# One recurrence, four engines: who takes the raw scores out of PSUM in the chunked RWKV-7 time mix

## What is computed

```python
def rwkv7_step(state, inp):
    r, w, k, v, a, bb = inp
    sa = jnp.einsum('bhij,bhj->bhi', state, a)
    state = (state * w[:, :, None, :] + sa[..., None] * bb[:, :, None, :]
             + v[..., None] * k[:, :, None, :])
    y = jnp.einsum('bhij,bhj->bhi', state, r)
    return state, y
```

## Time and profile before

| quantity | value |
| --- | --- |
| median of 3 runs | 3548.25 us |
| the profiled execution, its own time | 3558.19 us |
| its span in the profile | 3556.3 us |
| busy share of the span: TensorE, VectorE, ScalarE, GpSimd | 94%, 44%, 42%, 66% |
| mean granted clock of TensorE | 0.965 |
| recurrence (four chunks) | about 426 to 585 us |
| TensorE busy in one chunk of 38.8 us (third) | 29.7 us |
| GpSimd busy in the recurrence | 0 us |

### The profile page before, as it was taken

The page is one execution under the profiler, slowest core; times in us unless marked ns, Lnnn a source line. Parts: engine busy times, 40 slices in busy tenths (PEclk is TensorE's granted clock), DMA queues, the critical chain, the costliest instruction groups (busy, mean ns, idle before and its releaser), DMA issues.

```text
span 3556.3 us, 64623 instructions
## 1 busy us (share of the span) xinstructions
PE 3326.2 (94%) x23774; PEld 2994.4 (84%) x23774; DVE 1568.0 (44%) x2801; ACT 1476.6 (42%) x1933; POOL 2362.5 (66%) x1013
## 2 busy tenths in 40 slices
PE   7899878899999999888688999999999999999999
PEld 6798777888888888787677999998888888888899
DVE  2057755312221100369922495667741575137600
ACT  3255433444444333444344454343344334433433
POOL 5620101688888788553366787777788778877787
PEclk9999889999999999898899999999999999999999
DMA  5843301556555555443244555555555555655555
GB/s 179 194 151 129 109 3 61 155 173 187 184 187 184 174 186 184 132 130 95 71 136 144 164 183 166 170 171 154 176 171 186 172 173 161 194 177 172 159 183 165
DMA packets 158083, 555.26 MB, mean 156 GB/s; under 512 B 17248, under 2 KB 23584, under 8 KB 157840
## 3 DMA queue, kind: packets, MB, share of 16 engines
q1 hardware_dynamic: 151008, 540.08, 48.3%
q0 software_dynamic: 2192, 8.20, 1.3%
q10 hardware_dynamic: 4768, 5.36, 0.5%
HBM read 548.33 MB, written 5.24 MB: 156 GB/s over the span
## 4 chain that ended last, share of the span: by engine, by line
PE 74%; DVE 10%; POOL 8%; issue 7%; ACT 1%; POOLq 0%; DVEq 0%; ACTq 0%
PE ps L543 27%; PE ps L534 24%; PE ps L545 14%; POOL wl L482 8%; DVE ps L1704 2%; PE ps L743 2%; PE ps L612 1%; PE ps L936 1%; PE ps L570 1%; DVE arena L1673 1%; DVE misc L1671 0%; DVE under_u L1342 0%; DVE ehl L1841 0%; PE ps L621 0%; DVE arena L1495 0%
## 5 line engine op out<-in xcount | busy, mean ns | idle before, releaser
L482 POOL TENSOR_TENSOR wl<-raw,wh 128x1024 fp32r<-128x1024 f32 x984 | 2348.2, 2391 | 1059.7 <-ACT wh L1020 1059.6
L1020 ACT ACTIVATE wh<-raw 128x1024 fp32r<-128x1024 f32 (+1 forms) x1034 | 1087.1, 1053 | 1687.3 <-PE ps L545 1152.3
L543 PE MATMUL ps<-uhl,wh 128*128 128x512 f32 x3200 | 1140.9, 401 | 63.6 <-DVE uhl L1358 34.0
L534 PE MATMUL ps<-uhl,wh 128*128 128x256 f32 x4768 | 945.6, 289 | 19.4 <-DVE uhl L1358 9.9
L545 PE MATMUL ps<-uhl,wl 128*128 128x256 f32 x3200 | 903.6, 282 | 0.0
L534 PEld LDWEIGHTS ps<-uhl,wh 128*128 128x128 f32 x4768 | 777.0, 196 | 30.8 <-issue 12.4
L543 PEld LDWEIGHTS ps<-uhl,wh 128*128 128x128 f32 x3200 | 606.9, 190 | 215.7 <-DVE uhl L1358 35.2
L534 PE MATMUL ps<-uhl,wl 128*128 128x256 f32 x2640 | 754.6, 286 | 0.0
L545 PEld LDWEIGHTS ps<-uhl,wl 128*128 128x128 f32 x3200 | 610.7, 191 | 0.0
L543 PE MATMUL ps<-ehl,wh 128*128 128x512 f32 x1536 | 556.1, 402 | 9.2 <-DVE ehl L1841 5.6
L534 PEld LDWEIGHTS ps<-uhl,wl 128*128 128x128 f32 x2640 | 515.2, 195 | 0.0
(11 more groups left out here) (310 smaller groups left out, 2689.0 us busy)
## 6 DMA issues: line engine op xcount, KB each, us to landing
raw<-w_u SPq DMA_DIRECT2D x256, 512.0 KB, 3.5
raw<-w_v SPq DMA_DIRECT2D x256, 512.0 KB, 3.5
raw<-w_gu SPq DMA_DIRECT2D x176, 512.0 KB, 3.5
raw<-w_down SPq DMA_DIRECT2D x80, 512.0 KB, 3.6
raw<-w_out SPq DMA_DIRECT2D x64, 512.0 KB, 3.5
raw<-w_z SPq DMA_DIRECT2D x54, 512.0 KB, 3.7
raw<-w_in SPq DMA_DIRECT2D x52, 512.0 KB, 3.5
raw<-w_qkv SPq DMA_DIRECT2D x48, 512.0 KB, 3.6
```

Source lines behind the costliest of these rows:

```text
L482: pool.tensor_tensor(wl[:, slot, 0:width], raw[:, slot, 0:width], wh[:, slot, 0:width].bitcast(F32), ALU.subtract).then_inc(lo_ready, 1)
L534: ins = pe.matmul(out, w[:, slot, at], x(c), start=first and c == n == 0, stop=last and c == kt - 1 and n == 2)
L543: pe.matmul(bank(b).rearrange("p (n t) -> p n t", n=2), wh[:, slot, at], pair[:, :, k0 + c, :], start=first and c == 0, stop=False, skip_g ...
L1020: act.activation(wh[:, slot, 0:width], raw[:, slot, 0:width], ACT.Copy).then_inc(hi_ready, 1)
```

## The change

VectorE no longer masks the whole scores. It multiplies the near blocks straight from PSUM into `Bf[0]`, one instruction for each e over two banks, and then L727's product into `Bf[1]`. ScalarE waits for each of these near blocks and then copies the raw scores of that e, 128 x 1024, from PSUM to a new SBUF buffer `RAW`. It no longer makes the copy of v. GpSimd, between the fourth and the fifth split of `out`, runs a loop over the chunks: the identity added to the near blocks (`Bf[3]`), the far blocks (`Bf[2]`) from `RAW` in two instructions, the upper half of `QS` in two, the copy of v (not in the last chunk), and `MB` in two. TensorE gets waits at the places where each is first read, and `dve+` now takes its operand from the PSUM bank. `RAW` takes 2048 columns behind `MB`.

```diff
@@ -174,6 +174,7 @@
 ]
 PLUS_ID = {(2, 4), (6, 5)}
 NSTEP = len(INVERSE)
+FAR_STEP = min(n for n, step in enumerate(INVERSE) if any(2 in (a, b) for a, b, _, _ in step))
 
 
 MEAN_AT = (0, 2, 3, 5, 6, 8, 10, 11)
@@ -301,6 +302,7 @@
         o = temps
         QS = view(arena, o, NH, P); o += NH * P
         MB = view(arena, o, NH, P); o += NH * P
+        RAW = view(arena, o, 2, 8, P); o += 16 * P
         assert o <= temps_end, (o, temps_end)
         SV = view(xT_, 0, NH, CH)
         UV = view(xT_, 1024, NH, CH)
@@ -395,6 +397,9 @@
         p_ready, uh_ready = sem("p_ready"), sem("uh_ready")
         gp_ready, gh_ready = sem("gp_ready"), sem("gh_ready")
         gate_sum, up_sum, res_low, exp_sum = sem("gate_sum"), sem("up_sum"), sem("res_low"), sem("experts_sum")
+        scores_kept, near_in, near_id, far_in, qs_masked, v_low, mb_masked = (sem(n) for n in (
+            "scores_kept", "near_blocks", "near_plus_identity", "far_blocks", "reads_masked", "values_copied",
+            "keys_masked"))
         bk_tr, st_read, res_attn = sem("keys_turned"), sem("state_read"), sem("attention_added")
         mh_ready, ml_ready = sem("mixed_hi"), sem("mixed_lo")
         s_x = [sem(f"x_in{k}") for k in range(4)]
@@ -512,7 +517,31 @@
             for h in range(NH):
                 bias(h)
             pool.wait_ge(lo_ready, BASE["out"])
-            splits(BASE["out"], 32 + 176)
+            splits(BASE["out"], RING)
+            MB4, QS4 = (m.rearrange("p (k e) n -> p e k n", e=2) for m in (MB, QS))
+            wide = lambda m, n: m.unsqueeze(1).to_broadcast([CH, 8, n])
+            for c in range(NC_):
+                pool.wait_ge(near_in, 2 * c + 2)
+                pool.tensor_tensor(Bf[3], Bf[0], cst("i64").unsqueeze(1).to_broadcast([P, 8, CH]), ALU.add)\
+                    .then_inc(near_id, 1)
+                pool.wait_ge(near_id, c + 1)
+                for e in range(2):
+                    pool.wait_ge(scores_kept, 2 * c + e + 1)
+                    if e:
+                        pool.wait_ge(far_in, 2 * c + 1)
+                    pool.tensor_tensor(Bf[2][HD * e:HD * e + HD], RAW[0:CH, e, :, 0:CH], wide(cst("omask")[0:CH], CH),
+                                       ALU.mult).then_inc(far_in, 1)
+                pool.wait_ge(far_in, 2 * c + 2)
+                for e in range(2):
+                    pool.tensor_tensor(QS4[CH:P, e], RAW[CH:P, e], wide(cst("cmask")[CH:P], P), ALU.mult)\
+                        .then_inc(qs_masked, 1)
+                if c < NC_ - 1:
+                    pool.wait_ge(v_copied, c + 1)
+                    pool.tensor_copy(UV[CH:P, :, :], SV[CH:P, :, :]).then_inc(v_low, 1)
+                for e in range(2):
+                    pool.tensor_tensor(MB4[0:CH, e], RAW[0:CH, e], wide(cst("cmask")[0:CH], P), ALU.mult)\
+                        .then_inc(mb_masked, 1)
+            splits(BASE["out"] + RING, 32 - RING + 176)
             splits(BASE["down"], 96, 2 * DOWN_U, (DOWN_U - 1, 2 * DOWN_U - 1))
             splits(BASE["in2"], 4)
             pool.wait_ge(u_ready, 3 * DT)
@@ -720,7 +749,7 @@
                                         BK[hp:hp + HD, k, c, :], AR[hp:hp + HD, k, c, :], start=True, stop=True)
                     ins.then_inc(c_ps, 1)
 
-                pe.wait_ge(c_act, 5 * c + 2)
+                pe.wait_ge(c_act, 4 * c + 2)
                 for h in range(NH):
                     hp = HD * (h % 2)
                     k = h // 2
@@ -730,8 +759,13 @@
                 for n, step in enumerate(INVERSE):
                     if n == 0:
                         pe.wait_ge(c_dve, c + 1)
-                        pe.wait_ge(c_act, 5 * c + 5)
+                    if n == 1:
+                        pe.wait_ge(near_id, c + 1)
+                    if n == FAR_STEP:
+                        pe.wait_ge(far_in, 2 * c + 2)
                     for g in range(GROUPS):
+                        if n == 0 and g:
+                            pe.wait_ge(scores_kept, 2 * c + 2)
                         if evacuated(EVA, c, n, g):
                             pe.wait_ge(i_act, evacuated(EVA, c, n, g))
                         if evacuated(EVD, c, n, g):
@@ -748,6 +782,8 @@
 
                 if c:
                     pe.wait_ge(st_ev, c)
+                pe.wait_ge(c_act, 4 * c + 4)
+                pe.wait_ge(qs_masked, 2 * c + 2)
                 for g in range(GROUPS):
                     for h in range(8 * g, 8 * g + 8):
                         hp, k = HD * (h % 2), h // 2
@@ -766,11 +802,14 @@
                                         Bf[3][hp:hp + HD, k, :], start=True, stop=True)
                     ins.then_inc(v_ps, 1)
                 pe.wait_ge(uv_ev, GROUPS * (c + 1))
+                if c < NC_ - 1:
+                    pe.wait_ge(v_low, c + 1)
                 for h in range(NH) if c < NC_ - 1 else ():
                     ins = pe.matmul(bank(2 + h // 8)[0:CH, (h % 8) * CH:(h % 8 + 1) * CH], BKn[:, h, :],
                                     UV[:, h, :], start=True, stop=True)
                 if c < NC_ - 1:
                     ins.then_inc(n_ps, 1)
+                pe.wait_ge(mb_masked, 2 * c + 2)
                 for h in range(NH):
                     ins = pe.matmul(y_out(h), UV[0:CH, h, :], MB[0:CH, h, CH:P], start=False, stop=h >= NH - 2,
                                     skip_group_check=True)
@@ -1126,8 +1165,10 @@
                 for e in range(2):
                     act.activation(QS4[0:CH, e, :, :], AR4[HD * e:HD * e + HD, :, c, :], ACT.Copy)\
                         .then_inc(c_act, 1)
-                act.wait_ge(v_copied, c + 1)
-                act.activation(UV[CH:P, :, :], SV[CH:P, :, :], ACT.Copy).then_inc(c_act, 1)
+                for e in range(2):
+                    act.wait_ge(near_in, 2 * c + e + 1)
+                    act.activation(RAW[:, e], ps[:, 4 + 2 * e:6 + 2 * e, :].rearrange("p b (k n) -> p (b k) n", k=4),
+                                   ACT.Copy).then_inc(scores_kept, 1)
                 for n, step in enumerate(INVERSE):
                     for g in range(GROUPS):
                         half = slice(4 * g, 4 * g + 4)
@@ -1476,10 +1517,8 @@
             wend2 = wendh.rearrange("p (k e) n -> p e k n", e=2)
             dve.tensor_copy(wend2[0:HD, 0, :, :], wend[0:HD, :, :])
             link(dve.tensor_copy(wend2[0:HD, 1, :, :], wend[HD:P, :, :]))
-            MB4 = MB.rearrange("p (k e) n -> p e k n", e=2)
-            QS4 = QS.rearrange("p (k e) n -> p e k n", e=2)
             UV4 = UV.rearrange("p (k e) n -> p e k n", e=2)
-            cm, i64 = cst("cmask"), cst("i64")
+            i64 = cst("i64")
             for c in range(NC_):
                 dve.wait_ge(c_tr, c + 1)
                 if c == 0:
@@ -1490,23 +1529,12 @@
                 ins.then_inc(v_copied, 1)
                 for e in range(2):
                     dve.wait_ge(c_ps, 3 * c + e + 1)
-                    for b in range(2):
-                        src = bank(4 + 2 * e + b).rearrange("p (k n) -> p k n", k=4)
-                        dve.tensor_tensor(QS4[CH:P, e, 4 * b:4 * b + 4, :], src[CH:P], bc(cm[CH:P], CH, 4, P), ALU.mult)
-                        ins = dve.tensor_tensor(MB4[0:CH, e, 4 * b:4 * b + 4, :], src[0:CH], bc(cm[0:CH], CH, 4, P),
-                                                ALU.mult)
-                link(ins)
-                for e in range(2):
-                    ins = dve.tensor_tensor(Bf[0][HD * e:HD * e + HD], MB4[0:CH, e, :, 0:CH],
-                                            bc(cst("dmask")[0:CH], CH, 8, CH), ALU.mult)
-                link(ins)
-                dve.tensor_tensor(Bf[3], Bf[0], bc(i64, P, 8, CH), ALU.add)
+                    src = ps[0:CH, 4 + 2 * e:6 + 2 * e, :].rearrange("p b (k n) -> p (b k) n", k=4)
+                    dve.tensor_tensor(Bf[0][HD * e:HD * e + HD], src[:, :, 0:CH], bc(cst("dmask")[0:CH], CH, 8, CH),
+                                      ALU.mult).then_inc(near_in, 1)
                 dve.wait_ge(c_ps, 3 * c + 3)
                 dve.tensor_tensor(Bf[1], bank(0).rearrange("p (k n) -> p k n", k=8), bc(cst("dtmask"), P, 8, CH),
                                   ALU.mult).then_inc(c_dve, 1)
-                for e in range(2):
-                    dve.tensor_tensor(Bf[2][HD * e:HD * e + HD], MB4[0:CH, e, :, 0:CH],
-                                      bc(cst("omask")[0:CH], CH, 8, CH), ALU.mult)
                 for n, step in enumerate(INVERSE):
                     for g in range(GROUPS):
                         half = slice(4 * g, 4 * g + 4)
@@ -1517,10 +1545,10 @@
                                 src = bank(at + 4 * g).rearrange("p (k n) -> p k n", k=8)[:, half]
                                 dst = Bf[to][:, half]
                                 if engine == "act":
-                                    copied, done = dst, done + 1
+                                    done += 1
                                 elif engine == "dve+":
```

(2 more changed lines are left out.)

## The result

The changed kernel took 3522.78 us (median of 4 runs, 3518.23 to 3527.55) against 3547.57 us for the kernel before, run beside it: ratio 0.9929, 95% interval 0.991 to 0.9948. Two later series of six runs gave 0.9919 (0.989 to 0.9949) and 0.992 (0.9898 to 0.9942). The predicted 3526 us was 3 us too high.

A forecast was written before the change was run, and what follows sets the result against it. Bound: a latency chain in the recurrence, with an 8.42 us VectorE-to-TensorE handover per chunk. Handover 18.3 + clock 5.1 - waits 0.8 = 22.6 us off the 3548.25 us median: forecast 3526 us, range 3517 to 3540.

The forecast's parts named there:

- The likeliest case: Whole kernel: the recurrence's terms sum to 22.6 us off, giving 3526 us, chance 0.70.
- Handover: VectorE to TensorE ahead of the inverse: only three VectorE instructions stay, inverse 5.10 us earlier per chunk after the first.
- First chunk: Same handover with TensorE at the lower clock: inverse starts at 439.15 in place of 442.15, 3.00 us gained.
- Clock: First two inverse steps: TensorE's clock stays up through the shorter pause, 5.1 us gained, none in the first chunk.
- Rival A: Ahead of the inverse: the clock falls all the same, leaving 17.5 us of gain, 3530.7 us; chance 0.12.
- ScalarE's copy: Two 128 x 1024 copies of raw scores from PSUM, 1.06 us each; the second has 1.0 us of cover.
- GpSimd: Eight instructions per chunk, 15.9 us (16.3 with gaps), all hidden; the keys have 8.8 us to spare.
- Rival C: GpSimd far slower on these shapes, L775 waiting from 1.54 times on; at 2.5 times 3588 us; chance 0.04.
- `dve+`: Addition in the inverse reads PSUM instead of the SBUF copy: 0.42 us either way, zero gain.
- Rival B: GpSimd holds a port VectorE's evacuations of the inverse need, whatever their operands: 9.2 us slower, 3557; chance 0.05.
- six more waits on TensorE: Extra waits per chunk where TensorE first reads the new results: some 0.03 us each, 0.8 us lost in all.

The follow-up runs named there:

- before_filled2: Kernel before, plus matmuls of constants alternating between partition halves in TensorE's idle time ahead of the inverse; ratio 0.9975, recurrence 152.7 us.
- pool_plus8: Changed kernel with eight more 64 x 1024 masks on GpSimd per chunk ahead of the keys' masks; 3573.14 us in one run, recurrence 180.0 us.
- two_sbuf: Changed kernel with `dve+` reading ScalarE's copy from SBUF again, so with two SBUF inputs; 3540.34 us in one run, recurrence 142.7 us.

## Why the prediction was right

The likeliest case came true, and its terms can be set against the profile one by one.

1. Handover, chunks two to four: 5.10 us each predicted, 5.13 measured. The working held in its parts: near block 0.68 (0.70 assumed), the product 0.69, TensorE's own products as what is late next.
2. First chunk: 3.00 predicted, 3.03 measured.
3. Clock: 5.1 us predicted, 5.16 measured (0.05 + 1.97 + 1.13 + 2.01) in the first profile. The nothing that I gave the first chunk held there and in the second profile; in the third the clock happened to rise early, which gave another 4.4 us that no term covers. Step 2 follows step 0 by 5.84 us (473.41 to 479.25), 5.75 predicted. Rival A is out: the clock did not fall in the pause of 0.8 us, and `before_filled2` gets the same 5.1 us without the rest of the change.
4. ScalarE's copy: 1.02 us, 1.06 taken; it gated nothing. In the second chunk its second half ended at 473.31, ahead of the inverse.
5. GpSimd: 2.34 to 2.35 us for 64 x 1024 and 1.27 to 1.28 for 64 or 128 x 512, close to 2.41 and 1.29. Half the partitions are no cheaper. The copy of v took 1.05 us, not 2.41. So it was busy for 14.1 us per chunk where I had 15.9, and the keys had 10.8 us of room where I had 8.8. Rival C is out by these rows, and `pool_plus8` shows the deadline where the working puts it.
6. `dve+`: zero was right for the change as it is, and `two_sbuf` shows why: the old operand would have cost 11.8 us. Rival B, every operand held by GpSimd, is out (0.424 to 0.426 us in all 24, 18 of them beside GpSimd's work); its narrow form is real. The Trainium skill ("SBUF — State Buffer", Who interferes with whom) says that a VectorE instruction with two SBUF inputs contends with a GpSimd instruction that reads SBUF, and that one with a single SBUF input, outside the two-port modes, doesn't. These runs agree: 0.92 to 2.57 us for the 16 additions with two SBUF inputs that overlap a GpSimd instruction, 0.424 to 0.426 for the 18 with one.
7. The one term that was mis-sized: six more waits on TensorE, 0.8 us charged at 0.03 us each, a price that no row gave. The measured sum is 18.4 + 5.2 = 23.6 us, and the recurrence is 23.6 us shorter, so nothing is left over for them. From the inverse to the read of the state, where four of the six stand, it takes 17.96 us here and 17.96 in `before_filled2`, which has none of them. All of the difference between 22.6 and 23.6 is this term and the tenths above. The medians, by which the three series differ from the kernel before by 24.8 to 32.0 us, are too loose to test terms of this size.

What the prediction did not say is that GpSimd was dispensable. It argued that GpSimd's work is hidden, which is right, but it never asked whether VectorE had the room itself. Its own rows could have told: VectorE was busy for 21.18 of the third chunk's 38.80 us, so in a chunk of 32.5 us the same work leaves it 11 us idle.

## What to carry to other kernels

In a latency chain, ask of each instruction ahead of a handover whether the next engine needs its result now. Here only 3 of 12 were needed (two near blocks and the product), and moving the rest behind the signal was worth all of the gain, whichever engine did them, so long as they went into its idle time and not in one block. Copying the raw product out of PSUM once, on an engine with room, lets the masks come late. A pause of several us ahead of dense work on TensorE costs twice: here 5.93 us for the pause and 1.1 to 2.0 for the lower clock behind it.

## What the runs showed of the hardware

- Filler products of 64 x 64 whose operands and results stay in the same half of the partitions took 58 ns a record (9.7 us for 168). Alternating between the halves they took 30 ns (5.07 us for 168), with the clock at 1.0 in both. The first form also wrote the same columns each time and the second moved through eight places, so that it is the half that counts is not shown.
- A stage that no edit touches has two durations. The feed-forward stage `gu` took 477.0 us in six profiles and 486.2 in eight, with TensorE at full clock and busy for all but 0.8 us in both kinds. One window of 40 us of the changed kernel's first profile, then of its second (us, busy and count by engine, clock, DMA share, GB/s):

```profile
720.00:760.00 40.00, 40.00 (x229) 34.70 (x228) 8.30 (x15) 17.31 (x21) 33.99 (x15) 1.00 0.62 185
```

```profile
720.00:760.00 40.00, 40.00 (x233) 35.29 (x232) 8.30 (x15) 17.30 (x21) 34.86 (x15) 1.00 0.61 186
```

 The first has 229 matmul records in 40 us, the second 233. The cause stays open. It is a large part of why totals scatter by 20 us, with the expert stages (944 to 954 us for the long stretch) and the clock in the first chunk (0 to 4.6 us).
- In the first chunk TensorE was busy for 12 us without a pause at the lower clock in some executions, and in others the clock rose within the same work. With fillers ahead of it the clock did not fall at all, in all three profiles that had them.
